# Transposed banded attention: one first-look unit a step, a third rounded query buffer, value products of 512 columns

## The reference, cut to what matters

```
s_ctx = jnp.einsum('bnqhgd,bchd->bnhgqc', qb, kc).astype(jnp.float32) * GQA_SCALE
s_band = jnp.einsum('bnqhgd,bnkhd->bnhgqk', qb, kb).astype(jnp.float32) * GQA_SCALE
...
valid = (jnp.abs(qpos - kpos) <= WINDOW) & (kpos >= 0) & (kpos < n)
s_band = jnp.where(valid[None, :, None, None], s_band, -jnp.inf)
...
p = jax.nn.softmax(jnp.concatenate([s_ctx, s_band, s_sink], axis=-1), axis=-1).astype(v.dtype)
...
y_l = (windowed_gqa(q, k, v, ck, cv, sink_hg) * jax.nn.silu(g)) @ w_out
```

## Time and profile before

| | |
|---|---|
| median of 3 runs | 2806.09 us (2805.9 to 2808.06) |
| the profiled execution: its time, its span | 2809.59 us, 2807.8 us |
| busy share of the span | PE 92%, weight loads 72%, DVE 50%, ACT 41%, POOL 13% |
| mean granted clock of PE | 0.966 |
| first look of group 0 starts | 1178.68 us |
| the rows of group 0, of group 15 are transposed | 1191.0 us, 1490.3 us |

### The profile page before, as it was taken

How to read it: one execution, slowest core, us unless ns; L and a number is a source line. 1 busy time by engine, 2 the same in 40 slices (tenths; PEclk the granted TensorE clock), 3 DMA queues, 4 the chain that set the end, 5 groups by cost and what they waited for, 6 DMA issues and landing times. The chain is left out here.

```text
span 2807.8 us, 39492 instructions
## 1 busy us (share of the span) xinstructions
PE 2586.1 (92%) x15271; PEld 2016.2 (72%) x15271; DVE 1404.6 (50%) x2278; ACT 1154.4 (41%) x1977; POOL 371.0 (13%) x355
## 2 busy tenths in 40 slices
PE   5999999999999999888889999999898999999787
PEld 3778987877778888744446788877333887798776
DVE  5213266666655515655554723330677556364762
ACT  6112344544543321133443532220666647333662
POOL 1000020010020000035552000000000010004720
PEclk8999999999999999889999999999999999998889
DMA  7430000000123111100001320010100221111012
GB/s 262 166 135 23 30 21 1 1 1 1 61 72 109 37 47 31 69 1 1 1 1 64 110 83 31 1 60 31 45 1 20 78 79 46 38 46 60 1 53 76
DMA packets 75433, 139.97 MB, mean 50 GB/s; under 512 B 2841, under 2 KB 42162, under 8 KB 75122
## 3 DMA queue, kind: packets, MB, share of 16 engines
q1 hardware_dynamic: 58016, 75.89, 8.0%
q0 software_dynamic: 16992, 61.49, 6.1%
q10 hardware_dynamic: 242, 0.07, 0.0%
HBM read 120.67 MB, written 16.78 MB: 49 GB/s over the span
## 5 line engine op out<-in xcount | busy, mean ns | idle before, releaser
L171 ACT ACTIVATE WORK<-PS 128x512 f32<-128x512 f32 (+5 forms) x309 | 152.8, 495 | 660.4 <-PE PS L838 389.9
L838 PE MATMUL PS<-HT_R,W_R 128*128 128x512 f32 (+1 forms) x896 | 333.6, 372 | 0.0
L837 PE MATMUL PS<-WORK_R,W_R 128*128 128x512 f32 (+1 forms) x736 | 271.2, 368 | 0.0
L836 PE MATMUL PS<-WORK_R,W_R 128*128 128x512 f32 (+1 forms) x672 | 249.3, 371 | 14.4 <-DVE W_R L171 9.9
L171 ACT ACTIVATE HT<-PS 128x1024 f32<-128x1024 f32 (+6 forms) x211 | 156.2, 740 | 184.2 <-PE PS L1272 147.5
L964 PE MATMUL PS<-WORK_R,HT_R 128*128 128x512 f32 x528 | 210.2, 398 | 8.8 <-DVE W_R L171 7.5
L838 PE MATMUL PS<-W_R,WORK_R 128*128 128x256 f32 (+3 forms) x704 | 214.5, 305 | 0.0
L965 PE MATMUL PS<-WORK_R,MIXT_R 128*128 128x512 f32 x544 | 214.2, 394 | 0.0
L966 PE MATMUL PS<-W_R,HT_R 128*128 128x512 f32 x528 | 207.2, 392 | 0.0
L837 PE MATMUL PS<-W_R,HT_R 128*128 128x256 f32 (+2 forms) x688 | 206.1, 300 | 0.0
L901 PE MATMUL PS<-BASE,WORK 128*128 128x128 f32 (+1 forms) x1186 | 174.1, 282 | 23.3 <-DVE WORK L171 15.0
(11 more groups left out here) (330 smaller groups left out, 5671.9 us busy)
## 6 DMA issues: line engine op xcount, KB each, us to landing
MIXT<-in_w_mod POOLq DMA_DIRECT2D x8, 2048.0 KB, 8.9
x_scratch<-WORK POOLq DMA_DIRECT2D x24, 512.0 KB, 2.9
WORK<-x_scratch POOLq DMA_DIRECT2D x24, 512.0 KB, 3.6
W<-in_odd_w_in SPq DMA_DIRECT2D x12, 1024.0 KB, 5.1
W<-in_even_w_in SPq DMA_DIRECT2D x5, 2048.0 KB, 7.9
W<-in_w_mod SPq DMA_DIRECT2D x4, 2048.0 KB, 20.8
WORK<-in_x POOLq DMA_DIRECT2D x16, 512.0 KB, 8.0
W<-in_e_w_in SPq DMA_DIRECT2D x6, 1024.0 KB, 6.0
```

What stands on the lines that cost most here:

```text
L171: self.last = Signalled(self, issue(*args, **kwargs))
L836: mm(out, a[0], b_[0], start=k == 0, stop=False)
L837: mm(out, a[1], b_[0], start=False, stop=False)
L838: return mm(out, a[0], b_[1], start=False, stop=k == KT - 1)
```

## The change

It changes four things.

1. First look. A step now has one unit. Unit 0 of group `m + 2` stands at the end of the last step of group `m`, and units 1 to 4 of group `m + 1` stand in its first steps, each between scores and values. The rows move ahead of the values in the last step. Unit 0 of group 1 goes ahead of the loop.
2. As queries are needed a group earlier, there are three buffers `GQH`, and ACT rounds group `m + 2` where it rounded group `m + 1`.
3. The output of a group is laid out with the key head on partition halves, not the query head. So the values take two products of 512 columns instead of four of 256, the totals one of 512 and two of 512 instead of two and four of 256, and `SHIFT` has 512 columns instead of 768.
4. For that the gate's weight columns are loaded in another order, by four transfers of 256-byte rows instead of one of 1 KB rows, and the output weight's rows by four transfers of 64 partitions instead of one of 128. The four constant tables shrink.

The diff, cut to its core:

```
-CS_FOUR, CS_SINKS, CS_ROWS, NCS_ALL = 384, 1152, 1408, 1536
+CS_FOUR, CS_SINKS, CS_ROWS, NCS_ALL = 384, 896, 1024, 1152
...
+            in_parts[f"g_gate{m}"] = [(lambda v, i=i, a=a: v[:, :, P * i + 64 * a:P * i + 64 * a + 64],
+                                       cols(1536 + 512 * (m // 2) + 256 * a + 64 * (2 * (m % 2) + i), 64)) for i in range(2) for a in range(2)]
+        for n in range(2):
+            in_parts[f"o_out{n}"] = [(lambda v, a=a, g=g: v[64 * a:64 * a + 64, 4 * g:4 * g + 4, :],
...
+        def put_top(n, what):
+
+            slot = sum((n, x) in tops_in for x in range(3))
+            tops_in[n, slot] = what
+
+        tops_first = [("top", 0, u) for u in range(top_units(0))] + [("rows", 0, 0), ("top", 1, 0)]
         for m in range(len(groups) - 1):
-            n = first_step[m]
-            for u in range(top_units(m + 1)):
-                tops_in[n + 1 + u // 2, u % 2] = ("top", m + 1, u)
-            tops_in[last_step[m], 1] = ("rows", m + 1, 0)
+            for u in range(1, top_units(m + 1)):
+                put_top(first_step[m] + u - 1, ("top", m + 1, u))
+            put_top(last_step[m], ("rows", m + 1, 0))
+            if m + 2 < len(groups):
+                put_top(last_step[m], ("top", m + 2, 0))
...
-        SHIFT = [wide(HT_R, c, 0, 768) for c in (3, 6)]
+        SHIFT = [wide(HT_R, 3, 512 * n, 512) for n in range(2)]
...
-        GQH, GQL = [[wide(HT_R, c, 512 * n, 512) for n in range(2)] for c in (4, 5)]
+        GQH = [pair_of_heads(wide(HT_R, c, o, 512)) for c, o in ((4, 0), (4, 512), (6, 256))]
+        GQL = [pair_of_heads(wide(HT_R, 5, 512 * n, 512)) for n in range(2)]
...
-                    for i in range(2):
-                        last = mm(by_column_half(GOUT, par, i), VG[:, tiles[k], kv * GD:(kv + 1) * GD], head_halves(halves8(GPT[n % 3]), par, i),
-                                  start=k == 0 and par == 0, stop=k == len(tiles) - 1, skip_group_check=True)
+                    last = mm(GOUT[64 * par:64 * par + 64, :], VG[:, tiles[k], kv * GD:(kv + 1) * GD], GPT[n % 3][:, 512 * par:512 * par + 512],
+                              start=k == 0, stop=k == len(tiles) - 1, skip_group_check=True)
...
+                mm(GSUM, SINK_SUM_R, SHIFT[m % 2], start=True, stop=False, skip_group_check=True)
...
             gqa_rows(0)
+            gqa_top(1, 0)
...
                 gqa_tops(n, 1)
+                gqa_tops(n, 2)
...
             def group_high_parts(m):
-                if m >= 2:
-                    act.wait_ge(scored, 2 * (last_step[m - 2] + 1))
...
+                if m >= 3:
+                    act.wait_ge(scored, 2 * (last_step[m - 3] + 1))
...
-                    if k == 0 and m + 1 < len(groups):
-                        group_high_parts(m + 1)
-                    if k == 3 and m + 1 < len(groups):
+                    if k == 0 and m + 2 < len(groups):
+                        group_high_parts(m + 2)
+                    if m + 1 < len(groups) and k == top_units(m + 1) - 2:
                         gqa_sinks(m + 1)
```

More of the change, by code:

```diff
@@ L89, in shape_constants @@
     for n in range(4):
[L90 to L93, removed]
+        stage[:, CS_FOUR + n * P:CS_FOUR + (n + 1) * P] = ((row < 12) & (row % 4 == n))[:, None]
+    stage[:, CS_SINKS:CS_SINKS + P] = ((row >= 4) & (row < 12))[:, None] & (half[:, None] == block)
     stage[:, CS_ROWS:CS_ROWS + P] = (row < 4)[:, None]
@@ L389, in build @@
                 add(f"{name}{n}", rows_by_tile(w, 512 * n, 512 * n + 512))
[L390 removed]
+        for name, c0, n in [("g_kv", 1024, 2), ("g_gate", 1536, 4), ("g_q", 0, 4)]:
             for m in range(n):
@@ L423, in weights @@
             n = chunk_at[name]
-            loads = sum(len(src.shape) - 2 for _, src in chunks[n % WS:n + 1:WS] if src is not None)
+            loads = sum(len(in_parts.get(name_, [0])) for name_, src in chunks[n % WS:n + 1:WS] if src is not None)
             eng.wait_ge(w_in[n % WS], 16 * loads)
@@ L1263, in gqa_scores @@
                 kh, kl = KH2[:, gp, c], KL2[:, gp, c]
-                for step, (a_, b_) in enumerate(((kh, GQH[m % 2]), (kl, GQH[m % 2]), (kh, GQL[m % 2]), (FOUR_ROWS_R, SHIFT[m % 2][:, 0:512]))):
+                for step, (a_, b_) in enumerate(((kh, GQH[m % 3]), (kl, GQH[m % 3]), (kh, GQL[m % 2]), (FOUR_ROWS_R, pair_of_heads(SHIFT[m % 2])))):
                     if k == 0 and step == 0:
@@ L1271, in gqa_scores @@
                     for par in range(2):
-                        ins = mm(z[:, 512 * par:512 * par + 512], halves(a_, par), halves(b_, par), start=step == 0 and not banded,
+                        ins = mm(pair_of_heads(z[:, 512 * par:512 * par + 512]), halves(a_, par), halves(b_, par), start=step == 0 and not banded,
                                  stop=step == 3, skip_group_check=True)
@@ L1291, in gqa_top @@
                 bank = lambda par, c, n: TOPS[:, 512 * par + c:512 * par + c + n]
-                q = lambda par, i: halves(GQH[m % 2][:, i * P:(i + 1) * P], par)
+                q = lambda par, i: halves(GQH[m % 3][:, i // 2, (i % 2) * P:(i % 2 + 1) * P], par)
                 if u == 0:
@@ L1361, in gqa_totals @@
                     pe.wait_ge(mixed, m)
+                mm(GSUM, SINK_SUM_R, SHIFT[m % 2], start=True, stop=False, skip_group_check=True)
                 for par in range(2):
[L1363 to L1368, removed]
+                    last = mm(GSUM[64 * par:64 * par + 64, :], ONES[:, 0:64], psum_of(m)[:, par, :], start=False, stop=True, skip_group_check=True)
                 last.then_inc(totalled, 1)
@@ L1992, in group_high_parts @@
             def group_high_parts(m):
-                if m >= 2:
-                    act.wait_ge(scored, 2 * (last_step[m - 2] + 1))
-                for c, w, raw in group_raw(m):
-                    ins = f(GQH[m % 2][:, c:c + w], raw, ACT.Copy)
+                if m >= 3:
+                    act.wait_ge(scored, 2 * (last_step[m - 3] + 1))
+                for c, raw in group_raw(m):
+                    ins = f(GQH[m % 3][:, c], raw, ACT.Copy)
                 ins.then_inc(group_high, 1)
@@ L3285, in _ @@
                     sp.wait_ge(w_used, n - WS + 1)
[L3286 to L3290, removed]
+                for part, part_src in in_parts.get(name, [(lambda v: v, src)]):
+                    sp.dma_start(part(slot_view(n)), part_src).then_inc(w_in[n % WS], 16)
 _INS = ['x', 'c', 'ctx', 'c_ctx', 'w_mod', 'b_mod', 'norm_g', 'e_w_in', 'e_q_norm', 'e_w_qb', 'e_kv_norm', 'e_w_kvb',
```

41 lines of the change are left out of this document (22 added, 19 removed).

## The result

| | before | after |
|---|---|---|
| median of the runs | 2806.33 us (2805.9 to 2808.06, 4 runs) | 2782.94 us (2779.11 to 2783.48, 4 runs) |
| the profiled execution: its span | 2807.8 us | 2781.7 us |
| first look of group 0 starts | 1178.68 us | 1179.97 us |
| a group of five steps, 4 to 11 | 19.9 to 20.9 us | 18.87 us |

The ratio is 0.9913, interval 0.9895 to 0.9930: 23.4 us off the median and 26.1 off the profiled span. 2774 was forecast, 2760 to 2794 was the range. The time is inside it; the gain is three quarters of the 32.0 that were forecast.

What follows compares the result with a forecast made beforehand. It took two units in one step, with PE waiting for DVE's reductions, as the bound. Group terms summed to 267.3 us against 299.3, 32.0 less; from the median, 2806.1 - 32.0 = 2774 us, range 2760 to 2794.

Steps and rivals of the forecast that it cites:

- What bounds the stage: First look in the stage: PE waits 31.1 us for DVE reductions ahead of units; 2.64 us a group are lost.
- One unit a step: First look: units 1 to 4 don't wait; 0.29 us stays between unit 0 and unit 1, once a group.
- Rows ahead of the values: End of a group: POOL delays the transposition 0.7 us in groups 4 to 11, 5.6 us in all; bounds 0 and 1.45.
- the chain of 4.35: From unit 4 through reduction, maximum, ACT and last DVE product: 4.35 us with hand-over, before the transposition; slack 0.91.
- groups 12 to 14: Late groups of the stage: 17.55 us each for 12 and 13, 13.6 for 14, with nothing for POOL.
- Groups 0 and 1: First two groups of the stage: 17.7 and 19.8 us, at granted clocks of 0.50 up to 1200, then 0.83.
- Values and `SHIFT`: Values take 1.02 us a step (bounds 0.91, 1.13); `SHIFT` 0.64 to 0.96, no wait where covered, 0.80 where not.
- Loads and the third buffer: Gate chunk lands in 10 us (5.3 to 18), hidden by PE's work; third `GQH` buffer and earlier rounding cost nothing.
- Rival 1: POOL holds the row chain in all twelve groups of five steps, 1.45 us each: 2786 us, chance 0.18.
- Rival 2: Both DVE products on 8 columns meet a whole add, PE waits 3.8 us a group: 2823 us, chance 0.05.
- Rivals 3 and 4: Values: product count matters, 2760 us, chance 0.07; stage: another chain of about 19.9 us a group, 2806 us, chance 0.04.
- the signs that the prediction names: Stage trace: groups 17.3 to 18.3 us, unit 1 waits 0.3, values 1.02, transposition waits only in groups 4 to 11.

Runs made afterwards that it cites:

- late low parts: Changed kernel with POOL's two low parts of the output weight behind a group's last add instead of the second: 2775.58 us, ratio 0.9886 to the kernel before.

## Why the prediction was right, and where its sizes were off

**What bounds the stage: right.** Two units in one step were the bound. The old order of units with all the rest of the change gives the old time back, so the order is the whole measurable gain. This order has two moves, the units one to a step and the rows ahead of the values, and no run separates them; the waits say that the first won and the second gave a part back.

**One unit a step: right, with a small term too low.** The wait between unit 0 and unit 1 is 0.43, not 0.29, mostly because the unit takes 0.55 when scores follow it (1298.09 to 1298.64), where 0.65 had been read from one that values follow. The 0.14 in fourteen groups is 2 us, and the unit gives back 0.10 of it each time. Units 2 to 4 don't wait.

**Rows ahead of the values: the step that failed in size.** The prediction had a POOL add, made late by the low parts, hold DVE's row chain in groups 4 to 11, and took half of the bound: 0.7 us a group. The wait is 1.35, near the whole bound of 1.45. The mechanism and the groups were right, and two runs that moved only the low parts show it. What was wrong is the operation: not the last product, which meets a free POOL, but the first one, which starts 0.18 us after the add and so is held for nearly all of it. The slack was smaller as well: the maximum takes 0.79 there and not the 0.62 of the earlier trace rows. Together the two operations are 2.05 + 0.17 us longer than in the row that the chain of 4.35 was read from, which gives 4.35 + 2.22 - 5.26 = 1.31. That is 4.9 us of the miss. And the 487 ns of the earlier trace rows, which the prediction took for a sign of a hold in groups 4 to 11, came from elsewhere: from three holds of up to 2.15 us in groups 0, 13 and 14, none of which has low parts.

**The same hold in groups 12 to 14: missed.** They have no low parts, and the prediction had no wait there, though the last product of groups 13 and 14 was held in the kernel before. In group 13 the last product is the one that is held, by an add of POOL from 1444.17 on:

```profile
1444.17 4.84 POOL L169 TENSOR_TENSOR W<-W,HT 128x1024 f32<-128x1024 f32 x2 [3.06 <-ACT HT L169]
1444.32 2.22 DVE L169 TENSOR_TENSOR HT<-SMX,HT 128x8 fp32r<-128x8 f32 x1
...
1446.69 0.30 PE L1338 MATMUL PS<-BASE,HT 128*128 128x128 f32 x1 [2.21 <-DVE HT L169]
```

In group 12 the transposition waits 0.52, with another DVE operation of 1.22 us queued ahead of the last product. In group 14 it waits 1.81, as the first product is held there until an add ends (1460.77 and 1460.75). Behind the wait of group 13 the granted clock is 0.50 from 1447.3 to 1450.7, which is in its 19.5 us. Together these three groups are 3.9 us over the forecast. The waits and the clock cost more than that, as the forecast of group 13 kept a unit 4 (1.13 us: 1328.69 to 1329.82 before), which it doesn't have, since group 14 has four tiles. No run took these waits away by themselves.

**Groups 0 and 1: too high, by the clock.** The prediction carried over the granted clock of before, 0.50 up to 1200 and then 0.83. After the change it is 0.54 and 0.97, and between 1206 and 1223 it is 1.00, where before it was 0.84. That took 4.9 us off the two terms and gave 1.1 back in group 2, which has a stretch at 0.57 from 1225 to 1229. Before, PE stood 2.66 us for the rows at 1209.71 and 2.02 for a unit at 1220.68, and ran at half the clock behind both. After, it stands 1.91 at 1206.04 and keeps the full clock, and 1.26 at 1223.16, ahead of the stretch from 1225 on. With the old order of units the clock of 1200 to 1250 is 0.89, and the first two groups, from the first transposition, take 40.2 us against 32.6. The kernel before with the other gate loads has 0.89 and 40.1 as well, so 0.06 of the difference lies between two executions of one order. The rest, to the 0.97 of every run with the new order, came with the order of units; what in it raised the clock stays open, since no run changed that alone. The 1.91 at the end of group 0 had not been forecast, though the earlier trace rows has waits for the rows in four places and low parts stand in none of them; the first product is held there too (0.88). In group 1 unit 0 waits 0.79 for `SHIFT` (0.80 forecast), and the transposition 1.26 (0.76 forecast): the maximum takes 1.09 there, 0.47 over the 0.62.

**Values and `SHIFT`: right.** 1.01 to 1.02 us a step, and 0.69 us for 512 columns, near the low bound; only the two places without cover wait, 1.6 us in all.

**Loads and the third buffer: right.** No wait of PE for either. From the first issue to ACT's pass on gate chunk 1 it takes 6.8 us (976.91 to 983.72), where 10 had been taken for the load. The pass starts 2.8 us later than before, of which 1.3 is the shift of the whole execution.

**The rivals.** Rival 1, with a hold in all twelve groups of five steps, came nearer to the time (2786) than the likeliest value did, and by the medians the gain of 23.4 us lies in its band (8 to 24), 0.6 below the band of the forecast; the 26.1 of the profiled spans lies in the latter. The transposition waits in ten of its twelve groups, though the last product, which rival 1 names, is held in one of them alone (group 13); in groups 2 and 3 it waits for nothing. Rival 2 needed both products held for a whole add. The changed kernel holds the first for one, and the run with the low parts behind the third add holds three operations for 1.1 to 1.2 us each, and its groups are 19.1, still under 19.9. Rivals 3 and 4 are out by the products of 256 columns and by the time.

The Trainium skill (SBUF — State Buffer, SBUF: two separate sides) gives the rule behind the hold: of a DVE operation with two SBUF inputs and a POOL operation that reads SBUF, the one that starts first keeps the other out for its whole instruction. The traces agree: in the changed kernel all 24 held operations on 8 columns end 0.02 to 0.03 us behind the POOL operation that they met. In the kernel before, the add at 1469.56, which starts 0.22 behind a DVE product of 1.23 us with two SBUF inputs, takes 3.23 us instead of 2.36.

**The sum, and what was luck.** 4.9 for the low parts, 3.9 for groups 12 to 14, 1.0 net in groups 2 and 3, less 4.9 in groups 0 and 1, is but for rounding the 5.0 of 272.3 against 267.3. That the clock gave back 4.9 of the 8.8 us by which the holds passed the forecast was luck, as the prediction had carried the old clock over. The median missed 2774 by 8.9: 4.7 in the stage (27.3 us won, not 32.0), 1.2 by its later start, and nearly all of the rest because the profiled execution of before, from which the sum was taken off, lay 3.3 above its median, and that of after 0.5. Of the signs that the prediction names, the values step and the gate chunk came as told, and the waits ahead of unit 1 nearly so (0.43 and not 0.3). But ten of the twelve groups of five steps are longer than its 17.3 to 18.3 us, and the transposition waits outside groups 4 to 11 too.

## What to carry to other kernels

When the order on the bounding engine is tightened, the chain on the side engines becomes the next wait. Lay out where each small operation of that chain falls against the long operations of POOL, and cost a hold by where it starts, not by a mean. An operation that is longer in the row than its like may be a held one already: look for the operation of POOL that ends with it. A long POOL operation that nobody waits for belongs behind the chain's end, not ahead of the add that will meet it. And a price of a matmul group depends on its neighbours: read it from a pair in the new order.

## What was not expected of the hardware

A DVE operation on 8 columns takes 0.17 us alone and 2.22 when a POOL add of 2.37 starts just ahead of it: thirteen times as long. The reductions of DVE, whose only input is PSUM, aren't held: one of 1.23 us keeps its time when it starts 0.03 us after an add (1288.49 and 1288.52 above), and so do all 26 that start beside a POOL operation between 1195 and 1465 us in the changed kernel (1.22 to 1.23). When POOL has two operations back to back, DVE gets in between them and isn't held by both (three times in the run with the low parts behind the third add).

Whether the rest of the program runs a little faster or slower moves the time by up to some 6 us, with no change in it: from the first scores of group 15 to the end there are 1317.2 us in the changed kernel, 1319.9 with late low parts, 1320.1 and 1316.7 in the two runs with 256 columns, and 1314.3 with the low parts behind the third add. So differences under 6 us were read from the stage.
